# Building the expert gates of the dense tokens once per layer, with half of them kept in DRAM

## The reference, cut to what matters

```python
def block_fn(xb):                                     # tokens of one block
    q = (xb @ w_q).reshape(blk, PEER_HEADS, 2, PEER_HALF)
    s = jnp.einsum('thcd,hcnd->thcn', q, sub_keys)    # 2 x 128 key scores a head
    ...                                               # top 16 pairs of 8 heads
    expert = jnp.take_along_axis(cand_e, best_pos, axis=-1)     # 128 of 16384 a token
    gate = jax.nn.softmax(best_s, axis=-1)
    act = jax.nn.gelu(jnp.einsum('td,thkd->thk', xb, u[expert]), approximate=False)
    return jnp.einsum('thk,thkd->td', gate * act, v[expert])
```

## Time and profile before

| | |
|---|---|
| runs, us | 5728.08, 5732.89, 5743.93 |
| profiled execution, us | 5718.67 |
| its span, first to last instruction, us | 5716.5 |
| mean granted clock of TensorE | 0.838 of 2.4 GHz |
| busy share PE, DVE, POOL, ACT | 82%, 59%, 35%, 17% |
| expert stage, first layer | from about 1232 us to 2645 us |
| expert stage, second layer | from about 4281 us to 5690 us |

### The profile page before, as it was taken

How to read it: one execution, slowest core, us unless ns; L and a number is a source line. 1 busy time by engine, 2 the same in 40 slices (tenths; PEclk the granted TensorE clock), 3 DMA queues, 4 the chain that set the end, 5 groups by cost and what they waited for, 6 DMA issues and landing times. The chain is left out here.

```text
span 5716.5 us, 58737 instructions
## 1 busy us (share of the span) xinstructions
PE 4704.3 (82%) x20838; PEld 3520.9 (62%) x20838; DVE 3361.3 (59%) x8015; ACT 978.0 (17%) x1842; POOL 2024.9 (35%) x1580
## 2 busy tenths in 40 slices
PE   7888688839888898886886999776929988898887
PEld 5476366637565776654565888744719655585564
DVE  1324621996777887775138333243698677797775
ACT  0112200112111121111113222000103111121111
POOL 0000410212666446661014333130121666617663
PEclk9976788957999779998898888557966999969999
DMA  2421022114999759995110000102202999929998
GB/s 84 94 57 31 0 97 75 37 52 164 409 409 409 285 219 409 409 409 202 42 57 4 1 1 1 34 23 80 66 10 89 397 409 409 409 93 409 409 409 325
DMA packets 388116, 1076.15 MB, mean 188 GB/s; under 512 B 70092, under 2 KB 144557, under 8 KB 387366
## 3 DMA queue, kind: packets, MB, share of 16 engines
q0 software_dynamic: 184320, 671.17, 29.6%
q1 hardware_dynamic: 203510, 401.29, 19.8%
HBM read 1046.17 MB, written 29.30 MB: 188 GB/s over the span
## 5 line engine op out<-in xcount | busy, mean ns | idle before, releaser
L613 POOL DMA_INDIRECT fg_ug<-in_peer_u,f_idx x320 | 419.6, 1311 | 470.5 <-DVE fg_act_in L707 396.7
L613 POOL DMA_INDIRECT gg_ug<-in_peer_u,g_idx x320 | 401.7, 1255 | 437.5 <-DVE gg_act_in L707 369.7
L846 PE MATMUL fg_hid<-f_hT,fg_uT 128*128 128x256 f32 x2048 | 496.7, 399 | 0.0
L846 PE MATMUL gg_hid<-g_hT,gg_uT 128*128 128x256 f32 x2048 | 484.1, 391 | 0.0
L725 DVE SCALAR_TENSOR_TENSOR gg_xacc<-gg_vg,gg_wgt,gg_xacc 128x1024 f32<-128x1024 f32 x320 | 411.5, 1286 | 119.1 <-DMA gg_vg<-in_peer_v,g_idx 109.8
L855 PE MATMUL gg_out<-gg_dv,gg_pr 128*128 128x512 f32 x1024 | 462.8, 595 | 13.2 <-DVE gg_pr L692 13.1
L855 PE MATMUL fg_out<-fg_dv,fg_pr 128*128 128x512 f32 x1024 | 463.3, 595 | 4.6 <-DVE fg_pr L692 4.5
L725 DVE SCALAR_TENSOR_TENSOR fg_xacc<-fg_vg,fg_wgt,fg_xacc 128x1024 f32<-128x1024 f32 x320 | 412.3, 1288 | 69.7 <-DMA fg_vg<-in_peer_v,f_idx 62.8
L707 DVE CUSTOM_DVE_ANT_0 gg_junk<-gg_ug,gg_px 128x1024 f32<-128x1024 f32 x320 | 392.4, 1226 | 93.8 <-DMA gg_ug<-in_peer_u,g_idx 90.8
L846 PEld LDWEIGHTS fg_hid<-f_hT,fg_uT 128*128 128x128 f32 x2048 | 404.1, 203 | 56.5 <-issue 0.5
L620 POOL DMA_INDIRECT gg_vg<-in_peer_v,g_idx x320 | 365.0, 1140 | 187.6 <-DVE gg_xacc L725 105.3
(11 more groups left out here) (591 smaller groups left out, 8209.7 us busy)
## 6 DMA issues: line engine op xcount, KB each, us to landing
fg_du<-in_peer_u SPq DMA_DIRECT2D x128, 512.0 KB, 9.0
fg_dv<-in_peer_v SPq DMA_DIRECT2D x128, 512.0 KB, 6.8
gg_du<-in_peer_u SPq DMA_DIRECT2D x128, 512.0 KB, 9.0
gg_dv<-in_peer_v SPq DMA_DIRECT2D x128, 512.0 KB, 6.8
awg_wt<-in_mix_w_out SPq DMA_DIRECT2D x4, 2048.0 KB, 7.7
fs_wt<-in_peer_w_q SPq DMA_DIRECT2D x8, 1024.0 KB, 5.6
gs_wt<-in_peer_w_q SPq DMA_DIRECT2D x8, 1024.0 KB, 5.4
ap_wt<-in_mix_w_in SPq DMA_DIRECT2D x6, 1024.0 KB, 5.7
```

What stands on the lines that cost most here:

```text
L613: pool.indirect_dma_start(out=ug[:, n % NSLOT, :], out_offset=None, in_=u_rows, in_offset=bass.IndirectOffsetOnAxis(ap=index(n), axis=0)). ...
L846: last = pe.matmul(hid[:, b % 2, 0:DTOK], uT[:, b % 2, k, :], hT[:, k, DT0:DT0 + DTOK], start=(k == 0), stop=(k == KD - 1))
```

## The change

The gates of a token are made by one product of 128 columns, for all 128 blocks, ahead of block 0. ACT copies the first 64 blocks of the result to `gates` (now laid out by quarter, group of 8 tokens, block, token) and the other 64 to a small buffer `late`, two groups of 8 tokens deep. SP stores each group of `late` to a DRAM scratch. When the 16 blocks of a quarter of `gates` are used up, SP loads the late quarter into its place, in four pieces of 512 KB, one at each of four blocks. A PSUM bank now holds 4 tokens instead of 8. Beside that, DVE's products are written in place (over gl, and over the slot of ug), which frees pr and junk, and `dot` no longer waits for the dot before it.

```diff
-GB = 8
+GB = 4
 NGB = DTOK // GB
+TG = 8
+NTG = DTOK // TG
+QI = 16
+NQ = QBLK // QI
...
-        gates = ph.sb("gates", [P, QBLK, DTOK])
+        gates = ph.sb("gates", [P, NQ, NTG, QI, TG])
+        late = ph.sb("late", [P, 2, NQ, QI, TG])
...
-        ohi = ph.sb("ohi", [P, OHR, QBLK])
+        ohi = ph.sb("ohi", [P, OHR, P])
...
+                def gates_late(q, p):
+                    n = NTG // 4
+                    if p == 0:
+                        for c in range(2):
+                            sp.wait_ge(late_out[c], 16 * NTG // 2)
+                        sp.wait_ge(pr_done, QI * (q + 1))
+                    sp.dma_start(gates[:, q, n * p:n * (p + 1), :, :].rearrange("p g i t -> p g (i t)"),
+                                 g_dram[:, q, n * p:n * (p + 1), :]).then_inc(late_in[p], 16)
+
...
+                for g in range(NTG):
+                    sp.wait_ge(ev_done, GATE0 + 2 * (g + 1))
+                    sp.dma_start(g_dram[:, :, g, :], late[:, g % 2, :, :, :].rearrange("p q i t -> p q (i t)")
+                                 ).then_inc(late_out[g % 2], 16)
                 for b in range(NBLK):
+                    if QI <= b < QBLK + 4 and b % QI < 4:
+                        gates_late(b // QI - 1, b % QI)
                     if b + 2 < NBLK:
                         rows_u(b + 2)
...
-                def one_hots(q):
+                def one_hots():
                     for t in range(DTOK):
...
+                        if t >= OHR and t % GB == 0:
+                            dve.wait_ge(oh_used, (t - OHR) // GB + 1)
+                        dve.tensor_scalar(ohj[:, t % OHR, :], iota128, selT[:, 1, t:t + 1], None, ALU.is_equal)
+                        dve.tensor_scalar(ohi[:, t % OHR, :], iota_i[:, :], selT[:, 0, t:t + 1],
                                           selT[:, 2, t:t + 1], ALU.is_equal, ALU.mult).then_inc(oh_made, 1)
 
                 def product(b):
+                    q, i = b % QBLK // QI, b % QI
                     dve.wait_ge(gl_done, b + 1)
...
+                    if b == 0:
+                        dve.wait_ge(ev_done, GATE0 + NGB)
+                    if b >= QBLK and i == 0:
+                        for p in range(4):
+                            dve.wait_ge(late_in[p], 16 * (q + 1))
+                    g = gl[:, b % 2, :].rearrange("p (g t) -> p g t", t=TG)
+                    dve.tensor_tensor(g, g, gates[:, q, :, i, :], ALU.mult).then_inc(pr_done, 1)
...
-                    if g:
-                        dve.wait_ge(dot_done, g)
-                    dve.tensor_tensor_reduce(out=junk[:, :], in0=ug[:, g % NSLOT, :], in1=px[:, row_of[i], :],
+                    dve.tensor_tensor_reduce(out=ug[:, g % NSLOT, :], in0=ug[:, g % NSLOT, :], in1=px[:, row_of[i], :],
                                              scale=1.0, scalar=0.0, op0=ALU.mult, op1=ALU.add,
...
                 for b in range(NBLK):
-                    if b == QBLK:
-                        one_hots(1)
                     product(b)
...
+                def gates_out():
                     for j in range(NGB):
...
+                        n = GATE0 + j
+                        g, t = GB * j // TG, GB * j % TG
+                        made = pt[:, n % 2, :, :]
+                        act.wait_ge(oh_used, j + 1)
+                        act.activation(gates[:, :, g, :, t:t + GB].rearrange("p q i t -> p t q i"),
+                                       made[:, :, 0:QBLK].rearrange("p t (q i) -> p t q i", i=QI), ACT.Copy)
+                        if t == 0 and g >= 2:
+                            act.wait_ge(late_out[g % 2], 16 * (g // 2))
+                        act.activation(late[:, g % 2, :, :, t:t + GB].rearrange("p q i t -> p t q i"),
+                                       made[:, :, QBLK:P].rearrange("p t (q i) -> p t q i", i=QI), ACT.Copy
+                                       ).then_inc(ev_done, 1)
...
                     if b >= 2:
-                        act.wait_ge(pr_done, b - 1)
+                        act.wait_ge(o_done, b - 1)
                     act.activation(gl[:, b % 2, :], hid[:, b % 2, 0:DTOK], ACT.Gelu).then_inc(gl_done, 1)
...
+                def build():
                     for t in range(DTOK):
...
+                        n = GATE0 + t // GB
                         if t % GB == 0:
...
+                            pe.wait_ge(ev_done, n - 1)
+                        pe.wait_ge(oh_made, t + 1)
+                        last = pe.matmul(pt[:, n % 2, t % GB, :], ohj[:, t % OHR, :], ohi[:, t % OHR, :],
+                                         start=True, stop=True)
...
                 for b in range(NBLK):
                     if b + 1 < NBLK:
                         turn_rows(b + 1)
-                    if b == QBLK:
-                        output(b - 1)
-                        build(1)
-                        hidden(b)
-                        continue
                     hidden(b)
```

More of the change, by code:

```diff
@@ L522 @@
 OHR = 8
-GB = 8
+GB = 4
 NGB = DTOK // GB
+TG = 8
+NTG = DTOK // TG
+QI = 16
+NQ = QBLK // QI
 TB0 = DTILES + 2 * (GTILES + 1)
 def turn_batch(b):
-    return TB0 + 2 * b + NGB * (b >= 1) + NGB * (b >= QBLK + 2)
-def gate_batch(q):
-    return turn_batch(QBLK + 1) + 2 if q else turn_batch(0) + 2
+    return TB0 + 2 * b + NGB * (b >= 1)
+GATE0 = TB0 + 2
 def steps_of(b):
@@ L542, in uses, with peer_hybrid @@
     return layer * len(range(slot, NSET, NSLOT))
-def peer_hybrid(nc, name, layer, hT, sel, idx, u_rows, v_rows, u_tab, v_tab, x_dram, ident, iota128, u_in, v_in):
+def peer_hybrid(nc, name, layer, hT, sel, idx, u_rows, v_rows, u_tab, v_tab, x_dram, g_dram, ident, iota128, u_in, v_in):
     nu = len(UNITS)
@@ L556, in peer_hybrid @@
         gl = ph.sb("gl", [P, 2, DTOK])
-        pr = ph.sb("pr", [P, 2, DTOK])
         ug = ph.sb("ug", [P, NSLOT, D])
         vg = ph.sb("vg", [P, NSLOT, D])
-        junk = ph.sb("junk", [P, D])
         selT = ph.sb("selT", [P, 3, DTOK])
         ohj = ph.sb("ohj", [P, OHR, P])
-        ohi = ph.sb("ohi", [P, OHR, QBLK])
+        ohi = ph.sb("ohi", [P, OHR, P])
         iota_i = ph.sb("iota_i", [P, P])
@@ L582, in peer_hybrid @@
         oh_used = ph.sem("oh_used")
+        late_out = [ph.sem("late_out0"), ph.sem("late_out1")]
+        late_in = [ph.sem(f"late_in{p}") for p in range(4)]
         hid_done = ph.sem("hid_done")
@@ L740, in _ @@
                 dve.wait_ge(ev_done, DTILES)
-                one_hots(0)
+                one_hots()
                 dve.wait_ge(zeroed, 1)
@@ L766, in turned_rows @@
                         act.activation(uT[:, b % 2, 4 * c:4 * c + 4, :], pt[:, n % 2, :, :], ACT.Copy).then_inc(ev_done, 1)
-                def gates_out(q):
-                    if q:
-                        act.wait_ge(pr_done, QBLK * q)
+                def gates_out():
                     for j in range(NGB):
[L772 to L776, removed]
+                        n = GATE0 + j
[9 more added lines that the diff above has]
+                                       ).then_inc(ev_done, 1)
                 def dense_gelu(b):
@@ L800, in _ @@
                 turned_rows(0)
-                gates_out(0)
+                gates_out()
                 ready = {}
@@ L808, in _ @@
                         turned_rows(b + 1)
-                    if b == QBLK:
-                        gates_out(1)
                     dense_gelu(b)
@@ L827, in turn_rows @@
                         turn(turn_batch(b) + c, P, [du[:, b % 2, (4 * c + k) * P:(4 * c + k + 1) * P] for k in range(4)])
-                def build(q):
+                def build():
                     for t in range(DTOK):
-                        n = DTOK * q + t
-                        g = gate_batch(q) + t // GB
+                        n = GATE0 + t // GB
                         if t % GB == 0:
[L834 to L838, removed]
+                            pe.wait_ge(ev_done, n - 1)
+                        pe.wait_ge(oh_made, t + 1)
+                        last = pe.matmul(pt[:, n % 2, t % GB, :], ohj[:, t % OHR, :], ohi[:, t % OHR, :],
+                                         start=True, stop=True)
+                        if t % GB == GB - 1:
                             last.then_inc(oh_used, 1)
@@ L854, in output @@
                         for c in range(2):
-                            last = pe.matmul(out[:, r, 512 * c:512 * c + 512], pr[:, b % 2, r * P:(r + 1) * P],
+                            last = pe.matmul(out[:, r, 512 * c:512 * c + 512], gl[:, b % 2, r * P:(r + 1) * P],
                                              dv[:, b % 2, 512 * c:512 * c + 512], start=(b == 0), stop=(b == NBLK - 1))
@@ L865, in _ @@
                 turn_rows(0)
-                build(0)
+                build()
                 for b in range(NBLK):
@@ L889, in peer_ffn @@
         peer_hybrid(nc, name + "g", layer, hT, sel, idx, u.rearrange("l e d -> (l e) d"),
-                    v.rearrange("l e d -> (l e) d"), u[layer], v[layer], x_dram, ident, cst["iota128"], *rows_in)
```

(6 more changed lines are left out.)

## The result

The changed kernel takes **5582.26 us** (median of 4 runs, 5563.25 to 5600.59) against 5732.66 before: ratio 0.9735, 95% interval 0.9694 to 0.9775. That is 150 us less; the forecast was 5592 us, 141 less, with a range of 5552 to 5640.

The account below looks back on a forecast made before the run. The prediction took the DMA engines, at about 409 GB/s, to bound the steady expert stage. Its terms, -220 + 41 + 14 + 22 + 2 = -141 us, gave 5592 us on the median, range 5552 to 5640.

Parts of the forecast that it names:

- second build removed: Mid expert stage: removing the pause at the second gate build regains its lost DMA time, -220 us over both layers.
- read-back: Expert stage: loading the late gates costs its 8.39 MB per layer at 409 GB/s, +41 us for both layers.
- hole at the start: Build's start: the first late write lands behind SP's queued loads, stalling the build 11 us a layer, +22 us.
- pitch of the build: Gate build: DVE sets the pace with 128-wide one-hots, 0.453 us a token against 0.4266, +14 us over both layers.
- du block 2 later: After the build: SP issues this load only behind the last write, 1 us a layer, +2 us.
- the rest: Expert stage: strided gate reads, dropped waits between dots and dense_gelu's wait for output b-2 were each put at 0.
- SP's wait for product 16q+15: Before each quarter's first late load: over before SP gets there, 0, at most 4.5 us, four times.
- Rival A: Gate build: weight loads not hidden, PE sets the pace at 640 ns a token; 5688 us, chance 0.06.
- rival C: Gate build: late writes set the pace; equals the kernel before at a 9.9 us landing, up to 5802 us; chance 0.04.
- Rival D: Mid-stage: product 64 waits for late gates, so the pause stays; about 5733 us, chance 0.02.
- ACT's copies: Gate build: two copies per 4 tokens at 0.6 us each, 1.2 of 1.81 us, hidden under DVE.
- ACT's upper bound: Gate build: copies at their slowest take 2.1 us per 4 tokens, +18 us a layer, +36 in all.

Follow-up runs that it names:

- e4: Kernel before without its second gate build, blocks 64 to 127 weighted with the gates of blocks 0 to 63: 5519.97 us, ratio 0.9622.
- e1: The changed kernel run again with no edit, as a yardstick: 5588.71 us, ratio 0.9739 to the kernel before.
- e2: Changed kernel without the 16 loads of the late gates: 5534.18 us, ratio 0.9664 to the kernel before.
- e3: Changed kernel with SP's first late writes ahead of the xacc, du and dv loads, which follow singly behind writes 3 to 9: 5569.52 us, ratio 0.9722.
- e6: Changed kernel with PE multiplying only 64 of the 128 columns, all else kept: 5598.92 us, one run.
- e7: Changed kernel with DVE making the one-hots of j only for the first 8 tokens: 5503.24 us, one run.
- e8: Changed kernel with the wait between dots put back: 5584.5 us, ratio 0.9728 to the kernel before.
- e9: e3 with GpSimd instead of VectorE making the one-hot of j for every fourth token: 5544.56 us, ratio 0.967 to the kernel before.
- e5: Kernel before with only the in-place products and no wait between dots, two builds kept: 5724.48 us, ratio 0.9979.

## Why the prediction was right

The forecast was right in sign, in size and in most terms. Over both layers, in us, with what each term measured:

| term | forecast | measured | from |
|---|---|---|---|
| second build removed | -220 | -213.6 | e4 against before |
| read-back | +41 | +47.1 | e1 against e2 |
| hole at the start | +22 | +19.8 | builds of e1 against e3 |
| pitch of the build | +14 | +12.7 | builds of e3 against e4 |
| du block 2 later | +2 | +1.0 | PE's waits for it, 0.56 at 1385.65 and 0.47 in the second layer |
| the rest | 0 | about -13 | what is left of -146.2 (e1 against before) |

- **The pause** was priced in lost DMA time, and e4 bears that out. The price is 3% too high, all of it in the second layer; why stays open.
- **The read-back** costs its bytes at 409 GB/s plus 5.4 and 0.7 us, so "I take the bytes" is 6 us too low over both layers. In the middle of the stage the gathers cover the pieces, as forecast: PE waits longer, the DMA moves the same (e2). SP's wait for product 16q+15, put at 0 and at most 4.5 us, is 4.7 us, once.
- **The start** came out nearly to the microsecond when counted from the build's first product: the write was to land at +20.5 (1260 from 1239.46) and landed at +20.1 (1260.56 and 14.5 from 1254.97); DVE's wait is 10.7 us against 11. It came from one transfer's landing and from what SP's queue holds ahead of the write.
- **The pitch** of 0.453 us is 0.45 in the trace, and e6 and e7 show from both sides that DVE sets it. Rival A had rested on the clock staying at 1.2 GHz, and over most of the build it did not. But it is out at that clock too: in the 5.00 us at 0.50 behind the second layer's hole, at its 320 ns a product, PE would have got through some 16 products, not 24. So the rise of the clock is not what kept PE under DVE.
- **Writes** of 256 KB in 512 B runs landed in 2.6 us, where the forecast took 3.5; rival C needed 9.9. Rival D (pause at product 64) is excluded by the 409 GB/s of the middle.
- **ACT's copies** were taken at 0.6 us each and took 0.64 and 0.68, hidden under DVE as forecast.
- **What was missed:** about 13 us a kernel of gain that the forecast had at 0, in the small parts. They lie outside the builds, and e6 points to where most of them come from: the clock, which the forecast took to be 0.50. Without their builds, the stages of the six kernels that read back and whose build ends at 1.00 (after, e1, e3, e7, e8, e9) take 1222.9 to 1226.7 and 1215.1 to 1217.5 us; e6's, whose build ends at 0.50, take 1230.6 and 1219.9, 4.7 and 4.4 more than e1's. At the end of the build after, the clock is 1.00, and the products behind it run at the full rate from the first: hidden of block 0 takes 3.62 us. The same group behind the first build of the kernel before, and in e6:

```profile
1349.22 4.55 PE L846 MATMUL fg_hid<-f_hT,fg_uT 128*128 128x256 f32 x16
```
```profile
1378.44 5.49 PE L863 MATMUL fg_hid<-f_hT,fg_uT 128*128 128x256 f32 x16
```

This group alone is 0.9 to 1.9 us of it; how the rest of the 4 to 5 us a stage comes about is not shown, and e6 is a single run. e8 shows that it is not the dropped wait between dots. In the kernel before, the small edits alone gave 9 us (e5); there each stage has two ramps and a low clock. The 4 us that e6 leaves over may be their share, which no run takes apart.

The sum lay within 6 us of the -147 of the stages, partly because errors cancel: the pause gave 6.4 us less and the read-back cost 6.1 more than forecast, while the rest gave 13 more and the three small costs came out 4.5 lower. That the number came so close is in part luck. The range was wider than it had to be, mostly for ACT's upper bound.

## What to carry to other kernels

Price a pause in a stage that the DMA engines bound as the bytes that they did not move, and an added transfer there as its own bytes; both held to 15%. When a loop's first store shares a queue with a prologue's loads, issue the store first and hand the loads out between later stores: order alone gave back 8 to 9 us a stage (e3). When the profile's scatter lies outside the edited stage, count the stage, from the same instruction to the same instruction, not the span.

## What the runs showed of the hardware

- **The clock of the build rose.** With products of 128 columns PE was busy 96.87 of 100 us at a granted clock of 1.00, the level of 2.4 GHz (after); with products of 64, 89.67 of 90 us at 0.50, that of 1.2 (e6, and the earlier trace rows before).
- **At 0.50 a product of 128 columns takes no longer than one of 64:** 24 and 25 of them in 5.00 us (after, before).
- **A small write waits for the loads ahead of it:** the same 256 KB land in 2.6 us in the build, and in 14.5 behind the loads of xacc, du and dv in SP's queue.
- **A wait for the instruction before costs on the same engine too:** dots are 1.15 us apart without it (after) and 1.38 with it (e8).
- **GpSimd slows VectorE by 0.10 us** per one-hot of 0.78 us (e9).
